# A two-layer feed-forward, convolution and attention stack on one core: modulation's work moved between a quad's two pairs, and the first weight unit loaded ahead of the tokens

## The reference

```
def swiglu(h, w_gu, w_down):
    g, u = jnp.split(h @ w_gu, 2, axis=-1)      # w_gu 1024 x 5632
    return (jax.nn.silu(g) * u) @ w_down        # w_down 2816 x 1024

# second_block, for each of 2 layers l
cond = jax.nn.silu(c)                            # c: one row of 1024
mod = cond @ ada_w[l] + ada_b[l]                 # ada_w[l] 1024 x 3072
shift, scale, gate = jnp.split(mod, 3, axis=-1)
```

## Time and profile before

| | before |
|---|---|
| median of 3 runs | 1393.2 us (1391.09 to 1393.36) |
| the profiled execution's own time | 1391.8 us |
| span of its profile | 1390.0 us |
| ScalarE (ACT) busy | 806.5 us, 58% |
| VectorE (DVE) busy | 914.3 us, 66% |
| GpSimd (POOL) busy | 85.2 us, 6% |
| DMA | 240.01 MB, mean 173 GB/s |
| `w_lo` splits on VectorE | 376, 490.6 us |
| `w_hi` splits on ScalarE | 376, 411.9 us |
| modulation's scaling on ScalarE | 384 pieces, 117.6 us |

### The profile page before, as it was taken

One profiled execution on the slowest core, in us unless ns is written; L12 is line 12 of the kernel. 1 busy time (PEld: TensorE's weight loads), 2 busy tenths in 40 slices (PEclk: granted clock), 3 DMA queues, 4 the chain that ended last, 5 costly groups with the idle time before them and its releaser, 6 DMA issues.

```text
span 1390.0 us, 27578 instructions
## 1 busy us (share of the span) xinstructions
PE 1329.8 (96%) x10230; PEld 1284.1 (92%) x10230; DVE 914.3 (66%) x1514; ACT 806.5 (58%) x1570; POOL 85.2 (6%) x86
## 2 busy tenths in 40 slices
PE   6999999999999999999999999899999899999997
PEld 6999999998999999999999898799989899977887
DVE  5777636866777636777636776577764575566674
ACT  6666644446666636666645555576664443556673
POOL 2000011002000002000011000210001100000000
PEclk9999999999999999999999999999999999999999
DMA  5666654653766652766643432366675253345441
GB/s 194 238 228 236 236 175 139 183 166 95 250 229 233 242 167 66 249 227 236 238 155 109 124 112 71 122 204 231 230 260 179 77 167 107 114 156 157 136 123 46
DMA packets 63442, 240.01 MB, mean 173 GB/s; under 512 B 7120, under 2 KB 8576, under 8 KB 63232
## 3 DMA queue, kind: packets, MB, share of 16 engines
q1 hardware_dynamic: 63168, 238.84, 52.2%
q0 software_dynamic: 192, 0.04, 0.0%
HBM read 237.76 MB, written 1.05 MB: 172 GB/s over the span
## 4 chain that ended last, share of the span: by engine, by line
PE 85%; DVE 7%; ACT 4%; DMA 2%; issue 1%; POOL 0%; SPq 0%; ACTq 0%; DVEq 0%; POOLq 0%
PE bank L1805 22%; PE bank L1807 22%; PE bank L1806 22%; PE bank L1812 4%; DVE w_lo L1090 3%; PE bank L1813 2%; PE bank L1877 2%; PE bank L1878 1%; PE bank L1870 1%; ACT w_hi L597 1%; PE bank L2186 1%; DMA ada_raw<-ada_w 1%; DMA raw<-w 1%; ACT ada_raw L674 1%; ACT x_hl L629 1%
## 5 line engine op out<-in xcount | busy, mean ns | idle before, releaser
L1090 DVE TENSOR_TENSOR w_lo<-raw,w_hi 128x1024 fp32r<-128x1024 f32 (+2 forms) x376 | 490.6, 1308 | 319.6 <-ACT w_hi L597 318.9
L1805 PE MATMUL bank<-x_hl,w_hi 128*128 128x272 f32 (+1 forms) x1776 | 516.4, 291 | 16.0 <-DVE w_lo L1090 15.7
L1807 PE MATMUL bank<-x_hl,w_lo 128*128 128x272 f32 (+1 forms) x1776 | 510.9, 288 | 0.0
L1806 PE MATMUL bank<-x_hl,w_hi 128*128 128x272 f32 (+1 forms) x1776 | 509.1, 287 | 0.0
L597 ACT ACTIVATE w_hi<-raw 128x1024 fp32r<-128x1024 f32 (+2 forms) x376 | 411.9, 1101 | 119.6 <-PE bank L1807 102.6
L1805 PEld LDWEIGHTS bank<-x_hl,w_hi 128*128 128x128 f32 x1776 | 335.6, 189 | 18.8 <-DVE w_lo L1090 9.4
L1806 PEld LDWEIGHTS bank<-x_hl,w_hi 128*128 128x128 f32 x1776 | 338.3, 190 | 0.6
L1807 PEld LDWEIGHTS bank<-x_hl,w_lo 128*128 128x128 f32 x1776 | 335.2, 189 | 0.0
L1805 PE MATMUL bank<-a_hi,w_hi 128*128 128x272 f32 (+1 forms) x960 | 278.1, 290 | 12.2 <-DVE w_lo L1090 3.4
L1807 PE MATMUL bank<-a_hi,w_lo 128*128 128x272 f32 (+1 forms) x960 | 274.0, 285 | 0.0
L1806 PE MATMUL bank<-a_lo,w_hi 128*128 128x272 f32 (+1 forms) x960 | 273.4, 285 | 0.0
(11 more groups left out here) (282 smaller groups left out, 1414.9 us busy)
## 6 DMA issues: line engine op xcount, KB each, us to landing
raw<-w SPq DMA_DIRECT2D x312, 512.0 KB, 4.5
raw<-w SPq DMA_DIRECT2D x64, 704.0 KB, 4.6
ada_raw<-ada_w SPq DMA_DIRECT2D x48, 512.0 KB, 3.6
h<-x_in SPq DMA_DIRECT2D x1, 1088.0 KB, 5.2
work<-bands SPq DMA_DIRECT2D x1, 544.0 KB, 7.3
cst<-consts SPq DMA_DIRECT2D x1, 528.0 KB, 4.6
out<-h SPq DMA_DIRECT2D x1, 512.0 KB, 3.3
out<-h SPq DMA_DIRECT2D x4, 128.0 KB, 2.6
```

The lines of the kernel that those rows point to most:

```text
L1090: ve.tensor_tensor(w_lo[:, s, a:n], raw[:, s, a:n], w_hi[:, s, a:n].bitcast(F32), ALU.subtract).then_inc(w_lo_ready, 1)
L1805: te.matmul(dst, w_hi[:, s, a:a + P], rhs_hi, start=first, stop=False)
L1806: te.matmul(dst, w_hi[:, s, a:a + P], rhs_lo, start=False, stop=False)
L1807: return te.matmul(dst, w_lo[:, s, a:a + P], rhs_hi, start=False, stop=last)
```

## The change

It has four parts.

1. In `gu_quad`, ScalarE's scaling and VectorE's additions of a modulation unit move from the first pair to the place between the pairs: after `upper_a` and after `lower_a` of pair 0. The declared step lists follow.
2. SyncE issues the modulation unit between the second and the third transfer of a quad, and one quad later in the numbering, so that it still waits for the additions before. In the down projection units 10 and 11 are issued inside quads 0 and 1.
3. At the start SyncE issues weight unit 0, then the tokens as two transfers of 544 KB with a semaphore each, then units 1 to 3. ScalarE and VectorE split unit 0 ahead of their work on the tokens; ScalarE waits for each half of the tokens by itself.
4. TensorE's wait before the first unit of `dn` goes from step `lo0` to step `tg0` of the last turn.

```diff
-            act.phase(g, ["am", "silu0", "hi0", "silu1", "hi1"], 10)
-            vec.phase(g, ["tg0", "a0", "a1", "ar", "ur0", "full0", "lo0", "tg1", "ur1", "full1", "lo1"], 10)
+            act.phase(g, ["silu0", "hi0", "am", "silu1", "hi1"], 10)
+            vec.phase(g, ["tg0", "ur0", "full0", "lo0", "a0", "a1", "ar", "tg1", "ur1", "full1", "lo1"], 10)
...
             sp.dma_start(prm[:, :], params_in).then_inc(params_in_, 16)
-            sp.dma_start(h[:, :, :], x_in).then_inc(x_in_, 16)
...
-            def load(stage, i):
+            def load(stage, i, halfway=None):
...
                 for s in range(SLOTS):
+                    if halfway and s == 2:
+                        halfway()
                     if not (isinstance(i, int) and q == 0):
 
                         sp.wait_ge(w_lo_ready, SLOTS * q - SLOTS + s + 1)
+                    elif s == 1:
+                        for part, landed in ((slice(0, 4), x_in_), (slice(4, DC), x_in2)):
+                            sp.dma_start(h[:, part, :], x_in[:, part, :]).then_inc(landed, 16)
...
-                load(stage, 0)
+                if stage[:2] == "dn":
+                    load(stage, 0, lambda: load_ada(k, 10))
+                    load(stage, 1, lambda: load_ada(k, 11))
+                else:
+                    load(stage, 0)
                 if stage[:2] == "gu":
                     load_ada(k, 0)
-                if stage[:2] == "dn":
-                    load_ada(k, 11)
...
                 if stage[:2] == "gu":
                     load(stage, 1)
-                    load_ada(k, 1)
-                with sp.Fori(2 if stage[:2] == "gu" else 1, n) as i:
-                    load(stage, i)
-                    if stage[:2] == "gu":
-                        load_ada(k, i)
+                    load(stage, 2, lambda: load_ada(k, 1))
+                with sp.Fori({"gu": 3, "dn": 2}.get(stage[:2], 1), n) as i:
+                    load(stage, i, (lambda: load_ada(k, i - 1)) if stage[:2] == "gu" else None)
...
                 def gu_quad(i):
-                    ada(g, 12 * k + i)
                     for p in range(2):
                         split_next(g, i, 2 * p)
                         silu(g, p, i)
                         split_next(g, i, 2 * p + 1)
                         upper_a(g, p, i)
+                        if p == 0:
+                            ada(g, 12 * k + i)
...
-            sc.wait_ge(x_in_, 16)
-
+            split_hi("gu0", 0, 0)
             for c in range(DC):
+                if c % 4 == 0:
+                    sc.wait_ge((x_in_, x_in2)[c // 4], 16)
                 upper("pre0", c)
             for s in range(SLOTS):
-                split_hi("gu0", 0, s)
+                if s:
+                    split_hi("gu0", 0, s)
...
                         split_next(g, i, 2 * p)
-                        if p == 0:
-                            ada(g, i, i - 1, act.at(g, "am", i - 1))
                         ve.wait_ge(unit_done, SLOTS * q + 2 * p + 2)
...
                         lower_a(g, p, i)
+                        if p == 0:
+                            ada(g, i, i - 1, act.at(g, "am", i - 1))
...
+            split_lo("gu0", 0, 0)
             for c in range(DC):
                 lower("pre0", c)
-            for s in range(SLOTS):
+            for s in range(1, SLOTS):
                 split_lo("gu0", 0, s)
...
                             if s == 0:
-                                te.wait_ge(vec.sem, vec.at(g, "lo0", 9))
+                                te.wait_ge(vec.sem, vec.at(g, "tg0", 9))
```

More of the change, by code:

```diff
@@ L232, in build @@
         cum_in = sem("cum_in")
-        params_in_, x_in_, tables_in = sem("params_in"), sem("x_in"), sem("tables_in")
+        params_in_, x_in_, x_in2, tables_in = sem("params_in"), sem("x_in"), sem("x_in2"), sem("tables_in")
         act_b, vec_b, pe_b = (Steps(sem(n)) for n in ("scalar_softmax_steps", "vector_softmax_steps", "tensor_softmax_steps"))
```

## The result

The changed kernel takes 1375.9 us (median of 4 runs, 1374.9 to 1376.6), the kernel before beside it 1393.3 (1391.1 to 1394.2): a ratio of 0.9872, 95% interval 0.9858 to 0.9885. The forecast was 1377.5. The profiled execution has a time of 1375.94 us of its own and a span of 1374.1, so 15.9 us less than before against a sum of 14.7.

The account below looks back on a forecast made before the run. TensorE, busy 1329.8 of 1390.0 us, was taken as the bound, so only its idle time and matmul spacing could pay. Gains of 8.4 + 2.3 + 4.0 = 14.7 us gave 1377.1, a median of 1377.5 us, range 1373.5 to 1383.

Parts of the forecast that it names:

- The loop: In the `gu` turns: ScalarE and VectorE come round in 10.7 to 10.9 us instead of 11.48, under TensorE's time.
- Entry of `gu`: At quad 2 of each `gu`: four waits, 6.55 us, and `gu3`'s low clock go; net gain 8.4 us.
- the new wait of 1.3 us in `gu3`: At `gu3`'s entry: new waits of 0.2 us at unit 0 and 1.1 us at unit 2.
- pair 1 becomes the late one: Rival, chance 0.12: hand-overs cost 0.5 us more at four `gu` and four `dn` places: 1381.5 us.
- Entry of `dn`: At `dn3`, 3.7 us of waits and refills go; second units of all stages wait 1.4 us; net gain 2.3 us.
- The start: At the kernel's start: TensorE begins at 7.75 us instead of 12.25; gain 4.0 us, bounds 2.6 and 4.4.
- The wait of 0.45 us before unit 1: At the start: TensorE ends its first unit at 12.35 us, unit 1 is ready at 12.8, a 0.45 us wait.
- the clock stays low at the start: Rival, chance 0.09: after waiting behind its first unit TensorE runs another 16 matmuls slow, 0.1 us each: 1379 us.
- the lower bound of 2.6: At the start: if all transfers land together at 7.8 us, unit 1 is ready at 14.2, gain 2.6 us.
- Transfers in mid quad: In each turn: the modulation unit has 7 us against a median landing of 3.6 us; costs nothing.
- The "slower" rival: Rival, chance 0.03: modulation units land later than 7.8 us after `ar`; at 9.0, 43 us lost: 1420 us.
- The sum: Over the whole kernel: 8.4 + 2.3 + 4.0 = 14.7 us off the profiled 1391.8 us, giving 1377.1.

Follow-up runs that it names:

- The narrow additions: The changed kernel with GpSimd's additions over the squares cut to 8 of 272 columns: 1376.1 us, ratio 0.9877.
- the last-turn version: The changed kernel with the modulation in the last turn of each `gu` moved behind both pairs: 1372.5 us, ratio 0.9852.
- The third experiment: The kernel before with only TensorE's wait before `dn`'s first unit changed, `tg0` for `lo0`: 1395.3 us, ratio 1.0009.
- the second execution: The changed kernel measured and profiled once more with nothing altered: 1377.5 us, span 1375.9 us.
- the two other places: The changed kernel with the modulation transfer back in its old place: 1494.2 us; with it behind the quad's fourth weight transfer: 1461.8 us.
- the run where it happens: The changed kernel with the modulation unit issued behind its quad's fourth weight transfer instead of the second: 1461.8 us, ratio 1.0488.

## Why the prediction was right, point by point

**The loop.** Forecast 10.7 to 10.9 us early in a stage, measured 10.65 to 10.88; then TensorE's own 12.05. Right, and everything else hangs on it.

**Entry of `gu`.** All four waits went, as did the low clock in `gu3`. Of the new wait of 1.3 us in `gu3` only 0.51 came, at unit 2; the 0.2 at unit 0 did not. The working laid `gu1`'s rows on `gu3`, whose turns are shorter (10.7 us against 10.9); that this is the reason wasn't tried. The narrow additions, which take the wait away, show a part in it that the working left out: splits of 2.3 us beside GpSimd. Of the eight places of the rival "pair 1 becomes the late one", unit 2 was late in one `gu` of four; the four in `dn` waited about as the forecast itself had it.

**Entry of `dn`.** The waits of `dn3` went, and four came: 0.25 three times and 0.76, against 0.2 and 0.8. The waits came out better than their working. The last `lower_a` ends 12.8 us after the `gate` and not 13.3, and TensorE is there 0.5 us sooner than I had it, too. The two errors cancel, which is luck. In time they cost more than the 1.4 us of the sum: a wait of 0.25 lengthens its `dn` net by 0.49, the one of 0.76 by 1.00, together 2.4 (the last-turn version shows it). That is 1.0 more than forecast, and the new waits of `gu3` are about 0.8 less; in the sum the two nearly cancel. The third experiment shows that the changed wait is worth nothing with the old order: the time saved at the first unit is lost at the second, as the text said.

**The start.** 3.66 us by the first norm (3.44 in the second execution) against 4.0. The landings were right to 0.1 us in the profiled execution, and that was in part luck (see the end of this paragraph). The wait of 0.45 us before unit 1 did not appear, since TensorE was slower than I had it: the slow spacing lasts until 13.04, 21 intervals against 14 before, 0.7 us. That is the rival "the clock stays low at the start", half true: it took the place of the wait instead of adding to it. The landing in issue order holds, but not the time at which it begins: unit 0 was ready between 5.0 and 6.3 us in the ten profiles with this unit first in the queue, and in the nine of them with the tokens in halves the first half followed 1.2 to 1.6 us behind it. In these nine the first product starts between 7.9 and 9.2 us, three times after the 9 us that the forecast named as a sign of being wrong, and the first norm between 25.6 and 27.1. Against the 29.67 of before that is a gain of 2.6 to 4.1 us, so the 3.66 are near the better end, and the lower bound of 2.6 was reached without all transfers landing together. The Trainium skill's "DMA: Bandwidth & Descriptors", section "Queues, rings and completion order", says that completion is not first in, first out. No run here shows it at the start: in all thirteen profiles these transfers landed in the order of issue, units 1 to 3 1.2 to 1.3 us apart.

**Transfers in mid quad.** Costed at nothing, and nothing they cost: ScalarE waits for no modulation unit in any turn. The price of the two other places, 118 and 86 us above the changed kernel, shows how much hung on this choice. The "slower" rival had its mechanism right. Its price of 43 us was too low: in the run where it happens the turns are 1.3 us longer, near the 1.2 it took, but the lag then passes on to each `dn` net, whose second units wait 26.7 us in all, and in `gu3`, where TensorE needs only 11.4, each turn loses 2.4.

**The sum.** 15.9 us in the one execution and 14.1 in the other, 14.7 forecast. The medians give 17.4. Where the terms stand, the two executions have 14.4 and 13.7. What is over lies in the convolution part and in attention, which the change doesn't touch, and moves with the low clock's stretches from one execution to the next, so I don't credit it to the change. The same holds of the 1.0 us by which `gu2` with `dn2` beats its forecast in the first profile; the second has 1.01 against 1.2.

Two things stay open. What decides how long the low clock lasts in a given execution was not tried. And the last-turn version's gain over the changed kernel is shown in sign; of its 5.0 us the traces account for 2.4.

## What to carry to other kernels

When work is moved within a turn, ask what it frees and who stands in the queue behind it: the buffer that the additions free sets when its next transfer goes out, and a transfer that waits at the head of an in-order queue holds every transfer behind it. The whole change, start included, was worth -18 us against the kernel before with this transfer in the right place, +68 us with it half a quad later and +103 us with it in its old place, each by its ratio. A stage's last turn has other successors than the turns before it and deserves an order of its own. And before a difference of 1 to 3 us in one place is explained, look at the same kernel's second execution.

## What the hardware showed that I had not expected

- The time at the low clock level behind the same gap differs between executions: 15 long matmul intervals or 24 at the convolution part's first products, one or 16 behind the gap near 293 us, 1 to 2.6 us in one part of the kernel. The Trainium skill, in "TensorE: Matmul & The Clock Gate", section "What's actually happening", calls the number of slow matmuls at a kernel's start run-variable; these traces agree, and show it in mid kernel too.
- At the kernel's start the clock column prints 1.00 while 22 matmuls take 4.80 us. The spacing, not the column, tells the level there.
- VectorE's split of two SBUF tiles takes 1.8 to 3.1 us beside GpSimd's additions and 1.23 alone. The Trainium skill, in "SBUF — State Buffer", section "SBUF: two separate sides", has the two engines lock a shared port pair for whole instructions; the durations agree, and no run here tells a lock from a sharing.
- The same first weight transfer, in the same order of issue, was ready for ScalarE between 5.0 and 6.3 us in ten profiles.
- A wait of 0.25 us at the second unit of a `dn` net lengthens the net by 0.49 us, one of 0.76 us by 1.00.
